# One kernel for two transformer-like blocks: an empty bank turn moved behind the context tiles, and the lead-in's scale and shift sums shared out anew

## The reference, cut

```
c_act = jax.nn.silu(c)
mod = c_act @ mod_w[l] + mod_b[l]
shift, scale, gate = jnp.split(mod, 3, axis=-1)
h = rmsnorm(x, norm_g[l]) * (1.0 + scale[:, None, :]) + shift[:, None, :]
u = h @ w_in[l]
...
v = jax.nn.silu(layernorm(v, cln_g[l], cln_b[l]))
v = v @ pw2_w[l] + pw2_b[l]
y_conv = v * jax.nn.silu(cs)
...
y = jnp.concatenate([y_conv, y_lru], axis=-1) @ w_out[l]
x = x + (1.0 + gate[:, None, :]) * y
return rmsnorm(x, final_g)
```

## Time and profile before

| | us |
|---|---|
| median of 3 runs | 2104.98 |
| lowest and highest run | 2103.28, 2111.0 |
| the profiled execution, its own time | 2113.65 |
| its span, first to last instruction | 2111.9 |
| TensorE busy (share of the span) | 2026.9 (96%) |
| VectorE, ScalarE, GpSimd busy | 1244.7, 817.3, 992.3 |
| mean granted TensorE clock | 0.975 of full speed |

### The profile page before, as it was taken

One profiled execution on the slowest core, in us unless ns is written; L12 is line 12 of the kernel. 1 busy time (PEld: TensorE's weight loads), 2 busy tenths in 40 slices (PEclk: granted clock), 3 DMA queues, 4 the chain that ended last, 5 costly groups with the idle time before them and its releaser, 6 DMA issues.

```text
span 2111.9 us, 23938 instructions
## 1 busy us (share of the span) xinstructions
PE 2026.9 (96%) x9116; PEld 1672.2 (79%) x9116; DVE 1244.7 (59%) x1278; ACT 817.3 (39%) x1065; POOL 992.3 (47%) x559
## 2 busy tenths in 40 slices
PE   4999999999999999999999998988999999999998
PEld 3788788888787888878888887766788888778876
DVE  7889998887742375554511564489655555523126
ACT  4443346565542223321123464445343344502134
POOL 1274855555212222123321346647877877722254
PEclk7998999999999998999999999999999999999999
DMA  9541112121212333437854875341222222153133
GB/s 377 193 153 31 53 56 73 54 74 53 60 60 74 105 101 100 143 111 262 282 169 121 279 258 160 90 150 60 61 60 60 73 87 90 60 189 130 45 88 118
DMA packets 269247, 251.41 MB, mean 119 GB/s; under 512 B 8322, under 2 KB 230275, under 8 KB 269139
## 3 DMA queue, kind: packets, MB, share of 16 engines
q1 hardware_dynamic: 266051, 238.42, 35.9%
q10 hardware_dynamic: 3088, 11.54, 1.4%
HBM read 206.08 MB, written 43.84 MB: 118 GB/s over the span
## 4 chain that ended last, share of the span: by engine, by line
PE 69%; issue 16%; POOL 6%; DVE 5%; ACT 2%; DMA 2%; ACTq 0%; POOLq 0%; SPq 0%; DVEq 0%
PE PS L1724 34%; PE PS L2182 16%; PE PS L1965 5%; PE PS L2074 5%; POOL wl L840 3%; PE PS L2196 2%; PE PS L2018 1%; PE PS L2019 1%; PE PS L2027 1%; DVE SCR L2327 1%; POOL SCR L1030 1%; PE PS L1856 1%; DMA SCR<-in_ctx 1%; PE PS L2108 1%; POOL wl L1017 1%
## 5 line engine op out<-in xcount | busy, mean ns | idle before, releaser
L840 POOL TENSOR_TENSOR wl<-raw,wh 128x1024 fp32r<-128x1024 f32 (+1 forms) x157 | 380.3, 2423 | 829.1 <-ACT wh L1086 602.5
L1724 PE MATMUL PS<-XH,wh 128*128 128x512 f32 x1424 | 444.6, 394 | 9.6 <-POOL wl L840 3.1
L1724 PE MATMUL PS<-XH,wl 128*128 128x512 f32 x1424 | 442.5, 392 | 0.0
L1724 PE MATMUL PS<-XL,wh 128*128 128x512 f32 x1424 | 442.2, 392 | 0.0
L1724 PEld LDWEIGHTS PS<-XH,wh 128*128 128x128 f32 x1424 | 268.7, 190 | 69.7 <-issue 5.9
L1724 PEld LDWEIGHTS PS<-XH,wl 128*128 128x128 f32 x1424 | 269.8, 189 | 56.7
L1724 PEld LDWEIGHTS PS<-XL,wh 128*128 128x128 f32 x1424 | 269.7, 189 | 56.8
L1086 ACT ACTIVATE wh<-raw 128x1024 fp32r<-128x1024 f32 (+1 forms) x108 | 111.0, 1027 | 444.5 <-PE PS L1724 184.0
L2413 DVE SCALAR_TENSOR_TENSOR PS<-B,PJ,PS 128x1022 f32<-128x1022 f32 (+7 forms) x197 | 251.1, 1275 | 7.5
L1156 ACT ACTIVATE wh<-raw 128x1024 fp32r<-128x1024 f32 x48 | 50.8, 1058 | 265.4 <-PE PS L1724 248.1
L1017 POOL TENSOR_TENSOR wl<-SCR,wh 128x512 fp32r<-128x512 f32 x80 | 113.9, 1424 | 70.3 <-ACT wh L1552 69.8
(11 more groups left out here) (427 smaller groups left out, 3757.7 us busy)
## 6 DMA issues: line engine op xcount, KB each, us to landing
B<-in_ada_w SPq DMA_DIRECT2D x48, 512.0 KB, 5.4
raw<-in_ffn_up_w SPq DMA_DIRECT2D x48, 512.0 KB, 4.1
raw<-in_w_in SPq DMA_DIRECT2D x40, 512.0 KB, 4.7
raw<-in_m_in_w SPq DMA_DIRECT2D x37, 512.0 KB, 4.9
mod_tiles<-in_mod_w SPq DMA_DIRECT2D x16, 512.0 KB, 13.2
raw<-in_w_out SPq DMA_DIRECT2D x16, 512.0 KB, 5.0
qkvo_d<-B SPq DMA_DIRECT2D x16, 512.0 KB, 3.5
raw<-in_m_out_w SPq DMA_DIRECT2D x16, 512.0 KB, 4.1
```

What stands on the lines that cost most here:

```text
L840: tt(wl[slot][:, 0:kc, :], raw[slot][:, 0:kc, :], wh[slot][:, 0:kc, :].bitcast(F32), ALU.subtract).then_inc(lo_done, 1)
L1724: last = mm(ps[:, c:c + step_n], W[:, k, :], Y[:, k, c:c + step_n], start=(seen == 0), stop=(seen == total - 1))
```

## The change

The bank count: G1 counts eight tiles, and the empty tile stands behind the four of CX, so that everything from GxG on has the banks that it had. G2, G3 and CX swap banks.

The lead-in: c is loaded by itself, ahead of the other vectors, and TensorE transposes it after its fourth token tile; ScalarE forms silu(c) before its sixth square, the other three after the root as before. VectorE starts `mod_sum` before PV is copied and before the diagonals, and leaves out rows 2, 3 and 4 of scale (`BY_PE`). TensorE multiplies those three tiles by silu(c) directly, column by column, into the PSUM columns to which it then adds VectorE's sum of the other five; a product with a zero tile opens that group. MOD and SC of scale are formed as soon as the scale columns are there, and the first two tiles are scaled (`h_scaled`) before VectorE waits for the shift columns.

```diff
-        G1 = Product(KD, tiles=KD + 1)
+        G1 = Product(KD)
         G2, G3 = Product(KD), Product(KD)
-        CX = Product(HQ // P)
+        CX = Product(HQ // P, tiles=HQ // P + 1)
...
+        c_rows, C_PS = SCR[:, NST * P:(NST + 1) * P], PS[2][:, NST * P:(NST + 1) * P]
+        BY_PE = (2, 3, 4)
+        SCALE_PS, SHIFT_PS = PS[2][:, 0:KD], PS[2][:, SEQ // 2:SEQ // 2 + KD]
...
             sp.wait_ge(*at("stage_zero", 1))
+            sp.dma_start(c_rows[0:KD, :], A["c"][0].rearrange("(k p) -> k p", p=P)).then_inc(ev("c_in"), 16)
...
+            nc.gpsimd.memset(zero[:], 0.0).then_inc(step.sem, 1)
...
+                if c == 5:
+                    act.wait_ge(*at("c_ps", 1))
+                    f(CA[:, :, 0], C_PS[:, 0:KD], ACT.Silu).then_inc(ev("ca"), 1)
                 step.link(f(PS[3][:], B1[:, c, :] if c < NT else ctx_t[:, c - NT, :], ACT.Square, accum_out=small[:, 0, c:c + 1]))
...
-            for n, name in enumerate(("c", "c", "c_2", "c_ctx")):
+            for n, name in ((1, "c"), (2, "c_2"), (3, "c_ctx")):
...
-                if t == KD - 1:
-                    act.sem_inc(taken[1 - b], 1)
...
                 act.wait_ge(*at("kctx_sb", t + 1))
                 act.sem_inc(taken[b], 1)
+                if t == CX.n - 1:
+                    act.sem_inc(taken[1 - b], 1)
...
+                if c == 3:
+                    pe.wait_ge(*at("c_in", 16))
+                    nc.tensor.transpose(C_PS, c_rows, ident[:]).then_inc(ev("c_ps"), 1)
             pe.wait_ge(*at("stage_in", 16 * len(stage_rows)))
+            pe.wait_ge(*at("ca", 1))
...
+            def scale_columns(src, column, last=False):
+                for c in range(KD):
+                    ins = mm(SCALE_PS[:, c:c + 1], src[:, c * P:(c + 1) * P], column, start=False, stop=last and c == KD - 1)
+                return ins
+
+            def scale_tile(k):
+                pe.wait_ge(*at(f"mod_in{k // 2}", 32))
+                scale_columns(mod_t[:, k, :], CA[:, k, 0:1])
+
+            pe.wait_ge(*at("pv", 1))
+            mm(SCALE_PS, avg[:], zero[:], start=True, stop=False)
+            for k in BY_PE[:2]:
+                scale_tile(k)
             pe.wait_ge(*at("diag", 1))
...
-            pe.wait_ge(*at("pv", 1))
-            for q, (acc, c0) in enumerate(((T[4], KD), (T[0], 0))):
-                pe.wait_ge(*at("mod_sum", q + 1))
-                for c in range(KD):
-                    last = mm(MOD_PS[:, c0 + c:c0 + c + 1], acc[:, c * P:(c + 1) * P], ones[:], start=True, stop=True)
-                last.then_inc(ev("mod_sum_used"), 1)
+            for k in BY_PE[2:]:
+                scale_tile(k)
+            pe.wait_ge(*at("mod_sum", 1))
+            scale_columns(T[4], ones[:], True).then_inc(ev("mod_sum_used"), 1)
+            pe.wait_ge(*at("mod_sum", 2))
+            for c in range(KD):
+                last = mm(SHIFT_PS[:, c:c + 1], T[0][:, c * P:(c + 1) * P], ones[:], start=True, stop=True)
+            last.then_inc(ev("mod_sum_used"), 1)
...
+            BY_DVE = [[k for k in range(KD) if q or k not in BY_PE] for q in range(2)]
...
+            dve.wait_ge(*at("ca", 1))
+            mod_sum(0, 0)
+            dve.wait_ge(*at("stage_ps", 1))
+            V.tensor_copy(PV[:], PS[2][:, 0:NST * P]).then_inc(ev("pv"), 1)
+            mod_sum(0, 1)
+            dve.wait_ge(*at("rms", 1))
             diagonals(T[3], NT + NC, "diag")
...
+            for n in range(2, len(BY_DVE[0])):
+                mod_sum(0, n)
+            for n in range(len(BY_DVE[1])):
+                mod_sum(1, n)
+            dve.wait_ge(*at("mod_sum_used", 1))
+            step.link(V.tensor_tensor(MOD[:, KD:2 * KD], SCALE_PS, pvec("mod_b", 3 * KD)[:, KD:2 * KD], ALU.add))
+            step.link(V.scalar_tensor_tensor(out=SC[:, 0, :], in0=MOD[:, KD:2 * KD], scalar=1.0, in1=pvec("norm_g", KD), op0=ALU.add, op1=ALU.mult))
+            dve.wait_ge(*at("r_ps", 1))
+            dve.wait_ge(*at("ctxT_ps", 1))
...
+            for k in range(2):
+                h_scaled(k)
             dve.wait_ge(*at("mod_sum_used", 2))
...
+            step.link(V.tensor_tensor(MOD[:, 0:KD], SHIFT_PS, pvec("mod_b", 3 * KD)[:, 0:KD], ALU.add))
             dve.sem_inc(ev("mod_ok"), 1)
...
-            for k in range(KD):
+            for k in range(1, KD):
                 if k >= 2:
                     dve.wait_ge(*at("xl_L1", k - 1))
-                V.scalar_tensor_tensor(out=T[5 + k % 2], in0=B2[:, k, :], scalar=SC[:, 0, k:k + 1], in1=PS[3][:], op0=ALU.mult, op1=ALU.mult).then_inc(ev("h_t"), 1)
-                if k >= 1:
-                    h_low(k - 1)
+                    h_scaled(k)
+                h_low(k - 1)
             h_low(KD - 1)
```

More of the change, by code:

```diff
@@ L112, in block_pair_kernel @@
         share("dve_stage", *((n, 1) for n in ("stage_zero", "pv", "diag", "mod_ok", "pj", "sc_ok", "ln_diag", "n1_ms", "n1_diag", "n1_diag1", "n1_copy", "lf_sb", "rows_sb", "rec_zero", "h_rec0", "h_rec1", "n2_diag0", "n3_diag0", "n2_diag1", "n3_diag1", "n4_diag0", "n4_diag1")))
-        share("pe_stage", *((n, 1) for n in ("stage_ps", "r_ps", "ctxT_ps", "mean_ps", "var_ps", "ln_r", "stat1_ps", "n1_r2", "n1_r1", *(f"{n}{h}" for h in range(2) for n in ("n2_ps", "n3_ps")), "n4_ps0", "n4_ps1")))
+        share("pe_stage", *((n, 1) for n in ("c_ps", "stage_ps", "r_ps", "ctxT_ps", "mean_ps", "var_ps", "ln_r", "stat1_ps", "n1_r2", "n1_r1", *(f"{n}{h}" for h in range(2) for n in ("n2_ps", "n3_ps")), "n4_ps0", "n4_ps1")))
         share("act_stage", *((n, 1) for n in ("rms", "lam_e", "ctxn", "ln_sd", "n1_sd1", "n1_sd2", "f_e", "n2_sd0", "n3_sd0", "n2_sd1", "n3_sd1", "n4_sd0", "n4_sd1")))
@@ L131, in block_pair_kernel @@
             share(f"{a}_then_{b}", (a, n), (b, 0))
+        share("c_in_then_lf_out", ("c_in", 16), ("lf_out", 0))
         share("pool_stage", ("msum_zero", 1), ("pads_zero", 1))
@@ L182, in block_pair_kernel @@
         ones = sb("ones", [P, 1])
+        zero = sb("zero", [P, KD])
         small = sb("small", [P, 6, 16])
@@ L2299, in log1p @@
                 step.link(V.scalar_tensor_tensor(out=p, in0=s, scalar=2.0, in1=p, op0=ALU.mult, op1=ALU.mult))
-            V.memset(SCR[:, 0:NST * P], 0.0).then_inc(ev("stage_zero"), 1)
+            V.memset(SCR[:, 0:(NST + 1) * P], 0.0).then_inc(ev("stage_zero"), 1)
             for c in range(NT):
@@ L2304, in _ @@
                 V.tensor_copy(B2[:, :, c * P:(c + 1) * P], PS[c % 2][:].rearrange("p (k t) -> p k t", k=KD)).then_inc(ev("xT_sb"), 1)
-            dve.wait_ge(*at("stage_ps", 1))
-            V.tensor_copy(PV[:], PS[2][:, 0:NST * P]).then_inc(ev("pv"), 1)
-            dve.wait_ge(*at("rms", 1))
             dve.wait_ge(*at("consts", 3))
@@ L2315, in diagonals @@
                                 bc(small[:, 3, 0:NT], P), ALU.mult).then_inc(ev(event), 1)
-            diagonals(T[3], NT + NC, "diag")
-            def mod_sum(q):
-                o = (T[4], T[0])[q]
-                for k in range(KD):
[L2322 to L2330, removed]
@@ L2332, in _, with mod_sum @@
-            dve.wait_ge(*at("ca", 4))
-            for q in range(2):
-                mod_sum(q)
+            BY_DVE = [[k for k in range(KD) if q or k not in BY_PE] for q in range(2)]
+            def mod_sum(q, n):
+                o, k = (T[4], T[0])[q], BY_DVE[q][n]
+                t = KD * q + k
+                dve.wait_ge(*at(f"mod_in{t // 2}", 32))
+                if n == 0:
+                    ins = V.tensor_scalar(o, mod_t[:, t, :], CA[:, k, 0:1], None, ALU.mult)
+                else:
+                    ins = V.scalar_tensor_tensor(out=o, in0=mod_t[:, t, :], scalar=CA[:, k, 0:1], in1=o, op0=ALU.mult, op1=ALU.add)
+                if n < len(BY_DVE[q]) - 1:
+                    step.link(ins)
+                else:
+                    ins.then_inc(ev("mod_sum"), 1)
@@ new lines, in _, with h_scaled @@
+            step.link(V.tensor_tensor(MOD[:, KD:2 * KD], SCALE_PS, pvec("mod_b", 3 * KD)[:, KD:2 * KD], ALU.add))
+            step.link(V.scalar_tensor_tensor(out=SC[:, 0, :], in0=MOD[:, KD:2 * KD], scalar=1.0, in1=pvec("norm_g", KD), op0=ALU.add, op1=ALU.mult))
+            dve.wait_ge(*at("r_ps", 1))
+            dve.wait_ge(*at("ctxT_ps", 1))
+            def h_scaled(k):
+                V.scalar_tensor_tensor(out=T[5 + k % 2], in0=B2[:, k, :], scalar=SC[:, 0, k:k + 1], in1=PS[3][:], op0=ALU.mult, op1=ALU.mult).then_inc(ev("h_t"), 1)
@@ L2335, in _ @@
+            for k in range(2):
+                h_scaled(k)
             dve.wait_ge(*at("mod_sum_used", 2))
-            step.link(V.tensor_tensor(MOD[:, 0:2 * KD], MOD_PS[:, 0:2 * KD], pvec("mod_b", 3 * KD)[:, 0:2 * KD], ALU.add))
-            step.link(V.scalar_tensor_tensor(out=SC[:, 0, :], in0=MOD[:, KD:2 * KD], scalar=1.0, in1=pvec("norm_g", KD), op0=ALU.add, op1=ALU.mult))
+            step.link(V.tensor_tensor(MOD[:, 0:KD], SHIFT_PS, pvec("mod_b", 3 * KD)[:, 0:KD], ALU.add))
             dve.sem_inc(ev("mod_ok"), 1)
-            dve.wait_ge(*at("r_ps", 1))
@@ L2345, in h_low @@
```

(9 more changed lines are left out.)

## The result

The changed kernel took 2097.57 us (median of 9 runs, 2094.1 to 2098.82), the kernel before, run beside it, 2109.16 (9 runs, 2103.28 to 2112.55): a ratio of 0.9949, 95% interval 0.9937 to 0.9962, some 10.8 us or 0.51% less (the two medians lie 11.6 us apart). Run again later it gave 2095.1 against 2107.69, 0.9946 (0.9922 to 0.9971). The forecast was 2095.3 with 9.7 us gained. The total is close, and the parts under it were not all as forecast.

The account below looks back on a forecast made before the run. TensorE, busy 96% of the span, was taken as the bound, with time to win only at standstills or lower clock. Lead-in 5.8 plus bank count 3.9 gave 9.7 us: 2095.3 against the 2104.98 median, range 2089 to 2104.

Parts of the forecast that it names:

- The lead-in, forecast 5.8: Before TensorE's third unit: the first low part starts at 46.8 instead of 52.62 us, 5.8 us earlier.
- the shift run: TensorE's last one-column run in the lead-in, turning the shift sum into columns: from 41.6 to 45.2 us, 3.55 long.
- Rival 1: Lead-in: TensorE's clock stays low and its shift products end at 47.5; lead-in gain 3.5, total 7.4, 2097.6 us; chance 0.2.
- rival 4: Lead-in: one-column runs reading mod_w's tiles take twice 3.55 us; 6.8 us slower in all, 2111.8; chance 0.04.
- rival 3: Lead-in or G2: one of the two edits does nothing; 2101.1 or 2099.2 us; chance 0.1.
- MOD and SC take 0.6 us ... all under the shift run: VectorE's lead-in: with two tile scalings of 2.5 us, done at 44.7, hidden under TensorE's shift products.
- Rival 2: Lead-in: VectorE 1.7 us late, last sum waits for GpSimd; lead-in gain about 2.1, total 6.0, 2099.0 us; chance 0.08.
- the 2.0 us for the clash: Kernel before, lead-in: VectorE's last sum, held by GpSimd's low part, took 3.27 instead of 1.30 us; 2.0 us saved after.
- beside the shift: Lead-in: MOD, SC and two tile scalings, 3.1 us of VectorE work, hidden while TensorE does the shift products.
- The bank count, forecast 3.9: Hand-over from G1 to G2: standstill of 2.19 us and 1.70 of lower clock both vanish, 3.9 us.
- The 1.70 for the lower clock: Start of G2, behind the gap: 18 products took 5.80 us instead of 4.10; 1.70 us to be saved.
- rival 5: More than the sum: shift products at the upper clock too (1.7 us), or luckier clock in later one-column stretches; 2093.5; chance 0.12.

## Why the prediction was right, and where not

The time is within the forecast's range, and the gain is near the forecast's. The forecast gave most of its chances to a change that can't be told from none; with 9 runs of each kernel the interval of 0.38% to 0.63% does tell it.

**The lead-in, forecast 5.8.** The start of the sums, their end, the order on TensorE, the rise of its clock under the r product and the shift run came as forecast, the times within 0.5 us. Rival 1 (the clock stays low) and rival 4 (one-column runs from mod_w's tiles take twice as long) fell with the runs of 6.99, 1.84 and 1.93, and rival 3 (one edit does nothing) with the ratios of the two edits alone. Two terms were wrong, and both come from the same clash of VectorE with GpSimd.

The first is the step "MOD and SC take 0.6 us ... all under the shift run". SC reads two SBUF tiles and falls beside GpSimd's low part; it took 2.35 us, so the first low part came at 48.24 instead of 46.8, and of 5.8 us 4.4 were left. Rival 2 had the clash, but on the last sum and only for a late VectorE; the early one met it with its next step. Where SC went first by 10 ns, or read PSUM, it took 0.17 and the forecast's 46.8 and 74.1 were met within 0.35 us. The Trainium skill, "SBUF — State Buffer", section "Who interferes with whom", says that the pair of SBUF ports that the two engines share is an exclusive lock and that the order of issue decides who blocks; the runs agree on both, 2.35 against 0.17 us, with starts 20 ns one way and 10 the other. The forecast used that rule for the sums and not for the eight columns behind them.

The second is the 2.0 us for the clash in the kernel before. The last sum was held in one trace of three with that lead-in; the other two had their third unit at 77.75 and 77.81. So the change's gain at the third unit lies between 77.75 - 75.57 = 2.2 and 79.90 - 74.32 = 5.6 us, by which side of two such races an execution falls on. The forecast gave the upper end as the rule. Without the clash on either side the sums end only 1.2 to 1.3 us earlier (43.09 and 43.23 to 41.92), and the scalings put early, 1.6 to 1.7 us, are the largest single part.

"This is what 'beside the shift' hides: 3.1 us" was no term of the sum, and too large: the two scalings, 2.5 of it, cost 1.6 to 1.7 when they were put back, since the second one ran under ScalarE's pass anyway.

**The bank count, forecast 3.9.** The gap of 2.19 is gone wherever the edit is made and there in each of the three traces without it (both of before, and the lead-in alone). The 1.70 for the lower clock behind it was taken from the one trace of these that has it. GxG's wait is unaltered, so the empty tile behind the context costs nothing that the trace shows. Alone the edit gave 4.4 us with 1.3 to 7.4 as its interval.

**The rest.** With those corrections the path (the third unit and the gap at G2) gained 2.2 to 5.6 + 2.2, or 4.4 to 7.8 us by the traces; the two ratios say 10.8 and 11.4. What is missing is put down to TensorE's clock, as in rival 5; that is argued from means and not shown in the traces. The mean granted clock was 0.9783 over the 29 runs of before beside the first four experiments and 0.9806 over the 9 runs of after; 0.0023 x 2105 is 4.8 us, an estimate and an upper bound, since part of the time at the lower level lies in the lead-in, where TensorE waits anyway. In the later runs the same means are 0.9778 (21 runs) and 0.9804 (7 runs), so this wasn't one lucky set of executions.

Runs at one and the same clock split the gain: at 0.980 the few there are, seven and four of before, have mean spans of 2102.8 and 2102.1, three of after 2094.7, so some 7.4 to 8.1 us remain for the path, near the upper end of what the traces give. The lead-in alone has 0.9802 (12 runs), the bank count alone 0.9789 (12), the kernel without rows on TensorE 0.9791 (10): the higher clock goes with the new lead-in as a whole, and by which of its steps is open.

A single trace doesn't show it. The stretch from 154 to 174 us has 0.74 in the first trace of before and 0.91 in the first of after, 20 x 0.17 = 3.4 us of work. The one, then the other:

```profile
154.00:174.00 20.00, 20.00 (x93) 17.72 (x92) 19.43 (x17) 5.22 (x6) 9.24 (x5) 0.74 0.17 50
```

```profile
154.00:174.00 20.00, 20.00 (x97) 16.95 (x97) 19.33 (x17) 7.21 (x9) 7.82 (x4) 0.91 0.10 27
```

But the second trace of before has 0.91 there too, and the kernel with late scalings 0.74. So the forecast's gain was near partly by luck: its 9.7 us of path, over-counted by 1.9 to 5.3, were made up by more clock than the 1.70 that it counted.

## What to carry to other kernels

Beside a GpSimd instruction that reads SBUF, look at every VectorE step with two SBUF inputs, however small: eight columns cost 2.35 us instead of 0.17, and in the three traces that read one operand from PSUM that was gone, in two of them with GpSimd ahead. A stall in one profile that hangs on which of two engines starts first, here by 10 ns to 0.5 us, is a stall with a chance, so count it with that chance, and take a second profile before it goes into a sum as a constant. A delay or a gain of one or two microseconds ahead of a stretch in which TensorE's clock falls can be hidden there, since the falls differ by as much between executions, so such an edit is judged at the place where it acts and not by the total.

## What the runs showed of the hardware that was not expected

The same standstill of 2.19 us between two products was followed by a stretch at the lower clock in one execution (18 products in 5.80 us instead of 4.10) and by none in two others. The same run of 32 one-column products took 6.36 and 3.88 us in two executions of one kernel. Two executions of the kernel before came 10.2 us apart at GxG's opening, 2.1 of them from the order in which VectorE and GpSimd began. And two kernels whose third units start at 76.09 and 76.12, alike from there to G2, start G2 at 629.01 and 625.82.
